# A gated recurrence beside weight products: contributions in 64x64 array tiles and a gather by ScalarE

## The reference

```
q, k, log_f, v -> chunks of C = 32 tokens
b       = cumsum(log_f) in the chunk;  b_mid, b_last
scores  = (q * exp(b - b_mid)) @ (k * exp(b_mid - b))^T, lower triangle
o_intra = scores @ v
contrib = (k * exp(b_last - b))^T @ v             # 64 x 64 per chunk
decay   = exp(b_last)
state_n+1 = decay_n * state_n + contrib_n;  o_inter = (q * exp(b)) @ state_n
o = rmsnorm(o_forward + o_backward, norm_g) * silu(g)
```

## Time and profile before

| what | us |
|---|---|
| median of three runs | 1155.03 |
| the profiled execution | 1154.56 |
| its span, first to last instruction | 1152.7 |
| TensorE busy with matmuls | 1142.7 (99%) |
| VectorE busy | 621.3 (54%) |
| ScalarE busy | 455.0 (39%) |
| GpSimd busy | 82.2 (7%) |

### The profile page before, as it was taken

How to read it: one execution, slowest core, us unless ns; L and a number is a source line. 1 busy time by engine, 2 the same in 40 slices (tenths; PEclk the granted TensorE clock), 3 DMA queues, 4 the chain that set the end, 5 groups by cost and what they waited for, 6 DMA issues and landing times.

```text
span 1152.7 us, 16038 instructions
## 1 busy us (share of the span) xinstructions
PE 1142.7 (99%) x6071; PEld 922.9 (80%) x6071; DVE 621.3 (54%) x776; ACT 455.0 (39%) x682; POOL 82.2 (7%) x74
## 2 busy tenths in 40 slices
PE   9999999999999999999999999999999999999997
PEld 7888888888888777666788788888888888888886
DVE  6755555553333685444588956655455555542223
ACT  6423223232222445555757655534423223232223
POOL 0000000000001120000044320020000000000000
PEclk9999999999999999999999999999999999999999
DMA  6332232233323341211131122423232232232221
GB/s 206 110 109 92 90 109 91 98 126 100 101 86 130 127 132 58 71 55 55 55 111 39 57 74 92 164 94 108 92 109 91 91 109 87 95 102 99 92 92 73
DMA packets 31679, 111.59 MB, mean 97 GB/s; under 512 B 3984, under 2 KB 5136, under 8 KB 31376
## 3 DMA queue, kind: packets, MB, share of 16 engines
q1 hardware_dynamic: 30192, 104.11, 27.2%
q10 hardware_dynamic: 1440, 6.82, 1.6%
HBM read 105.41 MB, written 4.19 MB: 95 GB/s over the span
## 4 chain that ended last, share of the span: by engine, by line
PE 95%; DVE 2%; issue 1%; ACT 1%; DMA 0%; POOL 0%; ACTq 0%; DVEq 0%; POOLq 0%
PE ps L1166 26%; PE ps L1168 26%; PE ps L1167 26%; PE ps L1202 3%; PE ps L1201 3%; PE ps L1200 3%; PE ps L1306 1%; PE ps L1317 1%; PE ps L1332 1%; DVE w_lo L766 0%; PE ps L1461 0%; DVE k_sc L766 0%; DMA raw<-up_dram 0%; PE ps L1437 0%; PE ps L1366 0%
## 5 line engine op out<-in xcount | busy, mean ns | idle before, releaser
L1166 PE MATMUL ps<-h_hi,w_hi 128*128 128x512 f32 x1024 | 407.1, 398 | 0.0
L1168 PE MATMUL ps<-h_hi,w_lo 128*128 128x512 f32 x1024 | 398.9, 390 | 0.0
L1167 PE MATMUL ps<-h_lo,w_hi 128*128 128x512 f32 x1024 | 398.8, 389 | 0.0
L766 DVE TENSOR_TENSOR w_lo<-raw,w_hi 128x1024 fp32r<-128x1024 f32 (+2 forms) x190 | 236.1, 1245 | 191.9 <-ACT w_hi L411 185.7
L411 ACT ACTIVATE w_hi<-raw 128x1024 fp32r<-128x1024 f32 (+1 forms) x182 | 196.2, 1080 | 173.0 <-PE ps L1168 96.0
L1166 PEld LDWEIGHTS ps<-h_hi,w_hi 128*128 128x128 f32 x1024 | 192.2, 188 | 55.0 <-issue 15.8
L1167 PEld LDWEIGHTS ps<-h_lo,w_hi 128*128 128x128 f32 x1024 | 192.3, 188 | 41.6 <-issue 2.9
L1168 PEld LDWEIGHTS ps<-h_hi,w_lo 128*128 128x128 f32 x1024 | 192.2, 188 | 40.4
L481 ACT ACTIVATE g_hi<-un 128x512 f32 (+1 forms) x44 | 27.8, 632 | 250.8 <-DVE un L766 250.8
L766 DVE TENSOR_TENSOR un<-ps,rs 128x512 f32<-128x512 f32 x44 | 30.4, 691 | 122.2 <-PE ps L1168 122.2
L1166 PE MATMUL ps<-g_hi,w_hi 128*128 128x512 f32 x176 | 68.5, 389 | 0.0
(11 more groups left out here) (241 smaller groups left out, 1188.0 us busy)
## 6 DMA issues: line engine op xcount, KB each, us to landing
raw<-up_dram SPq DMA_DIRECT2D x86, 512.0 KB, 3.2
raw<-proj_dram SPq DMA_DIRECT2D x26, 512.0 KB, 3.2
raw<-down_dram SPq DMA_DIRECT2D x16, 704.0 KB, 4.1
raw<-down_dram SPq DMA_DIRECT2D x22, 512.0 KB, 3.2
raw<-gates_dram SPq DMA_DIRECT2D x16, 512.0 KB, 3.2
raw<-branch_dram SPq DMA_DIRECT2D x8, 512.0 KB, 3.2
raw<-wout_dram SPq DMA_DIRECT2D x8, 512.0 KB, 3.2
x_spill_dram<-xT ACTq DMA_DIRECT2D x1, 2048.0 KB, 7.0
```

The costliest lines, as they stand in the source:

```text
L766: return V.tensor_tensor(out, a, b, op)
L1166: T.matmul(ps[:, bank, :], w_hi[:, slot, cols], moving_hi(j), start=start and j == 0, stop=False)
L1167: T.matmul(ps[:, bank, :], w_hi[:, slot, cols], moving_lo(j), start=False, stop=False)
L1168: ins = T.matmul(ps[:, bank, :], w_lo[:, slot, cols], moving_hi(j), start=False, stop=stop and j == tiles - 1)
```

## The change

The zeros in `k_nat` go: one buffer, filled by one copy of 128 partitions from bank 7. contributions takes 64 rows of tokens by 64 columns and writes banks 6 (even super-chunks) and 7 (odd), dense. A new ScalarE step, contributions_to_sbuf, copies both halves into `con_sb` in the interleaved order, and the scan reads that. The step is placed ahead of exponentials(u+2). On ScalarE keys_to_sbuf moves ahead of norm_exp; on VectorE query_key of the even tiles from 4 on moves between the first and second product of normalize; on GpSimd the far queries become a step of their own behind key_to_end, and gate_outputs waits until the queries for the edges are made. The output banks are 4 and 5.

```diff
-        k_nat = [at("k_nat0", 80, [P, ST, P]), at("k_nat1", 88, [P, ST, P])]
+        k_nat, con_sb = at("k_nat", 80, [P, ST, P]), at("con_sb", 88, [P, HD * NSUP])
-        OUT_BANKS = (5, 7)
+        OUT_BANKS = (4, 5)
 # GpSimd
             def query(u):
-                pool.wait_ge(qs_done, u + 1)
-                pool.wait_ge(fac_done, u + 1)
-                late = 1 - u % 2
-                nc.gpsimd.tensor_tensor(kq_far[:, :, late, :], ...).then_inc(qfar_done, 1)
+            def far_query(u):
+                late = 1 - u % 2
+                pool.wait_ge(qs_done, u + 1)
+                nc.gpsimd.tensor_tensor(kq_far[:, :, late, :], ...).then_inc(qfar_done, 1)
-            for masked in k_nat:
-                nc.gpsimd.memset(masked[:], 0.0).then_inc(zero_done, 1)
                 query(u + 1)
                 key_to_end(u + 1)
+                far_query(u + 1)
                 if u and u % 2 == 0:
+                    pool.wait_ge(qe_done, 2 * u + 4)
                     gate_outputs(u // 2 - 1)
 # ScalarE, keys_to_sbuf
-                for b, tokens in enumerate(head_rows):
-                    A(k_nat[b][tokens, :, :].rearrange("p j c -> p (j c)"), ps[tokens, 6, :], ACT.Copy).then_inc(kn_done, 1)
+                A(k_nat[:].rearrange("p j c -> p (j c)"), ps[:, 7, :], ACT.Copy).then_inc(kn_done, 1)
+
+            def contributions_to_sbuf(u):
+                act.wait_ge(con_done, u + 1)
+                if u:
+                    act.wait_ge(state_done, u)
+                A(con_sb[:].rearrange("p (e j b) -> p b j e", j=ST, b=2),
+                  ps[:, 6:8, 0:S // 2].rearrange("p b (j e) -> p b j e", e=HD), ACT.Copy).then_inc(ccp_done, 1)
...
             keys_to_sbuf(0)
             exponentials(1)
+            contributions_to_sbuf(0)
...
+                if u + 1 < TILES:
+                    keys_to_sbuf(u + 1)
                 if u and u % 2 == 0:
                     norm_exp(u // 2 - 1)
-                if u + 1 < TILES:
-                    keys_to_sbuf(u + 1)
...
                 if u % 2:
                     outputs_to_sbuf(u // 2)
+                if u + 1 < TILES:
+                    contributions_to_sbuf(u + 1)
                 if u + 2 < TILES:
                     exponentials(u + 2)
 # VectorE
                 link(stt(o_u[:], o_u[:], -0.5, o_ms[:], ALU.mult, ALU.mult))
+                if u is not None:
+                    query_key(u)
                 link(stt(o_rs[:], o_u[:], 1.5, o_rs[:], ALU.add, ALU.mult))
...
-                dve.wait_ge(con_done, u + 1)
+                dve.wait_ge(ccp_done, u + 1)
-                con, flat = ps[:, 4, :], ...
+                con, flat = con_sb[:], ...
...
-                if odd and u + 1 < TILES:
+                if u == 1:
                     query_key(u + 1)
...
-                    normalize(t - 1)
+                    normalize(t - 1, u + 2 if u + 2 < TILES else None)
 # TensorE
             def mean_square(t):
-                pe.wait_ge(kn_done, 2 * min(2 * t + 3, TILES))
+                pe.wait_ge(ccp_done, min(2 * t + 3, TILES))
             def key_transposes(u):
-                if u >= 3 and u % 2:
-                    pe.wait_ge(oeps_done, u // 2)
                 if u:
-                    pe.wait_ge(kn_done, 2 * u)
+                    pe.wait_ge(ccp_done, u)
-                    ins = T.transpose(ps[:, 6, ...
+                    ins = T.transpose(ps[:, 7, ...
             def contributions(u):
-                pe.wait_ge(kn_done, 2 * u + 2)
+                pe.wait_ge(kn_done, u + 1)
-                if u:
-                    pe.wait_ge(state_done, u)
+                if u >= 3:
+                    pe.wait_ge(oeps_done, (u - 1) // 2)
-                    j = n // 2
+                    j, tokens = n // 2, head_rows[n % 2]
-                        ins = T.matmul(ps[rows, 4, :].rearrange("p (e n) -> p e n", n=NSUP)[:, :, n],
-                                       k_nat[n % 2][:, j, HD * a:HD * (a + 1)], v_h[:, j, HD * h:HD * (h + 1)], start=True, stop=True)
+                        ins = T.matmul(ps[rows, 6 + n % 2, HD * j:HD * (j + 1)],
+                                       k_nat[tokens, j, HD * a:HD * (a + 1)], v_h[tokens, j, HD * h:HD * (h + 1)], start=True, stop=True)
```

More of the change, by code:

```diff
@@ L219, in build @@
         sc_done, scm_done, kt_done, kn_done = sem("sc_done"), sem("scm_done"), sem("kt_done"), sem("kn_done")
-        zero_done, con_done, state_done = sem("zero_done"), sem("con_done"), sem("state_done")
+        zero_done, con_done, ccp_done, state_done = sem("zero_done"), sem("con_done"), sem("ccp_done"), sem("state_done")
         o_done, osq_done, oms_done = sem("o_done"), sem("osq_done"), sem("oms_done")
@@ L338, in query @@
                 nc.gpsimd.tensor_tensor(q_sc[:], q_sc[:], hq[:, u // 2, :], ALU.mult).then_inc(qs_done, 1)
-                pool.wait_ge(qs_done, u + 1)
-                pool.wait_ge(fac_done, u + 1)
-                late = 1 - u % 2
-                nc.gpsimd.tensor_tensor(kq_far[:, :, late, :], supers(q_sc[:])[:, :, CHUNK * late:CHUNK * (late + 1)],
-                                        far_q[:, u % 2, :].unsqueeze(2).to_broadcast([P, NSUP, CHUNK]), ALU.mult).then_inc(qfar_done, 1)
             def key_to_end(u):
@@ L355, in key_to_end @@
                                         .to_broadcast([P, 2 * NSUP, CHUNK]), ALU.mult).then_inc(ke_done, 1)
+            def far_query(u):
+                late = 1 - u % 2
+                pool.wait_ge(qs_done, u + 1)
+                nc.gpsimd.tensor_tensor(kq_far[:, :, late, :], supers(q_sc[:])[:, :, CHUNK * late:CHUNK * (late + 1)],
+                                        far_q[:, u % 2, :].unsqueeze(2).to_broadcast([P, NSUP, CHUNK]), ALU.mult).then_inc(qfar_done, 1)
             def gate_outputs(t):
@@ L367, in _ @@
             key_to_end(0)
+            far_query(0)
             pool.wait_ge(sil_done, HH)
             pool.wait_ge(pv_done, PAIRS)
-            for masked in k_nat:
-                nc.gpsimd.memset(masked[:], 0.0).then_inc(zero_done, 1)
             pool.wait_ge(spilled, 16)
@@ L672, in keys_to_sbuf @@
                     act.wait_ge(con_done, u)
-                else:
-                    act.wait_ge(zero_done, 6)
-                for b, tokens in enumerate(head_rows):
-                    A(k_nat[b][tokens, :, :].rearrange("p j c -> p (j c)"), ps[tokens, 6, :], ACT.Copy).then_inc(kn_done, 1)
+                A(k_nat[:].rearrange("p j c -> p (j c)"), ps[:, 7, :], ACT.Copy).then_inc(kn_done, 1)
[5 more added lines that the diff above has]
+                  ps[:, 6:8, 0:S // 2].rearrange("p b (j e) -> p b j e", e=HD), ACT.Copy).then_inc(ccp_done, 1)
             def outputs_to_sbuf(t):
@@ L684, in outputs_to_sbuf @@
                     for j, from_rows in enumerate(head_rows):
-                        A(out[:, :, j, :, :], ps[from_rows, OUT_BANKS[0]:OUT_BANKS[1] + 1:2, P * a:P * (a + 1)]
+                        A(out[:, :, j, :, :], ps[from_rows, OUT_BANKS[0]:OUT_BANKS[1] + 1, P * a:P * (a + 1)]
                           .rearrange("p b (q c) -> p q b c", c=SUPER), ACT.Copy).then_inc(ocp_done, 1)
@@ L1023, in cumulate, with normalize @@
                 tt(chunks(k_sc[u % 2][:]), b3, mid.unsqueeze(2).to_broadcast([P, 2 * NSUP, CHUNK]), ALU.subtract).then_inc(d1_done, 1)
-            def normalize(t):
+            def normalize(t, u=None):
                 dve.wait_ge(oy_done, t + 1)
                 link(stt(o_u[:], o_u[:], -0.5, o_ms[:], ALU.mult, ALU.mult))
+                if u is not None:
+                    query_key(u)
                 link(stt(o_rs[:], o_u[:], 1.5, o_rs[:], ALU.add, ALU.mult))
@@ L1075, in scan_states @@
                 turn = slice(None, None, -1 if u % 2 else 1)
-                con, flat = ps[:, 4, :], state[u % 2][:].rearrange("p e n -> p (e n)")
+                con, flat = con_sb[:], state[u % 2][:].rearrange("p e n -> p (e n)")
                 V.tensor_tensor_scan(flat[:, turn], decay[u % 2][:, turn], con[:, turn], 0.0, ALU.mult, ALU.add).then_inc(state_done, 1)
@@ L1398, in key_transposes @@
                 pe.wait_ge(ke_done, u + 1)
-                if u >= 3 and u % 2:
-                    pe.wait_ge(oeps_done, u // 2)
                 if u:
-                    pe.wait_ge(kn_done, 2 * u)
+                    pe.wait_ge(ccp_done, u)
                 for j in range(ST):
-                    ins = T.transpose(ps[:, 6, P * j:P * (j + 1)], k_end[:, P * j:P * (j + 1)], ident)
+                    ins = T.transpose(ps[:, 7, P * j:P * (j + 1)], k_end[:, P * j:P * (j + 1)], ident)
                 ins.then_inc(kt_done, 1)
```

## The result

The changed kernel is slower, not faster: a median of 1160.2 us over 5 runs (1159.3 to 1160.67) against 1154.86 for the kernel before on the same chip. The ratio is 1.0045 with a 95% interval of [1.0034, 1.0055], so 5.3 us more where 4.8 less were forecast. Its profiled execution has a span of 1158.4 us against 1152.7: 5.7 more. The predicted time and its range were missed, on the other side of no change. Medians and ranges here are those of undisturbed executions; one of e4's ten took 2324.3 us and is left out.

The account below looks back on a forecast made before the run. TensorE, 99% busy, was taken as the bound. Gains of 2.70 + 0.29 + 0.49 + 1.63 = 5.11 us less 0.3 of new wait gave 4.8 net, from 1155.03 to a median of 1150.2 us; range 1148.8 to 1153.4.

Parts of the forecast that it names:

- Contributions on TensorE: The 64x64 contributions in the recurrence gain 0.46 us in tile 0 and 0.32 in each of seven others, 2.70 together.
- Rival B: Change of matmul form eats the contributions' gain in all tiles; 2.1 us gained, 1152.9 us; chance 0.14.
- The second copy of the keys: One 128-partition key copy ahead of norm_exp removes TensorE's waits for `k_nat` in tiles 0, 2 and 4: 0.78 us.
- The wait for `k_end`: query_key inside normalize makes `k_end` ready near 631.4, removing TensorE's waits in tiles 3 and 5: 1.63 us.
- The copy: ScalarE's new contributions_to_sbuf, 128x512 per tile, takes 0.60 us and stays hidden from TensorE.
- hidden, by 0.6: mean_square, wanted at 618.76, finds ScalarE's copy done by 618.2, so it does not wait.
- What is late next: VectorE: VectorE's run to the end of scan_states(3) ends at 633.77, a new wait of 0.3 us before outputs(3), bounds 0 to 1.5.
- the split: VectorE's split beside GpSimd's multiplication took 2.20 instead of 1.2; with gate_outputs held back, that 1.0 us goes.
- the last two products of normalize: VectorE's two products beside GpSimd's queries, 1.02 against 0.69 each, are spared some 0.7 us.
- Once only: The 0.3 us wait occurs only before outputs(3); outputs(5) has a whole gate unit before it, outputs(7) no cumulation.
- C: VectorE and ScalarE become the bound: slow forms stay, copy takes 1.0; 2.0 us lost, 1151.9 us; chance 0.16.
- D: ScalarE's strided copy is slow and delays exponentials and transposes; eats the 4.8 us gain at 1.9; chance 0.08.

Follow-up runs that it names:

- e4: Changed kernel with mask copy of odd tiles ahead of normalize, their scan inside it behind query_key, yb_hi and yb_lo moved: 1156.03 us, ratio 1.0013.
- e2: Kernel before with only the three moves (keys_to_sbuf, query_key, far queries with gate_outputs' wait); 128-row contributions and PSUM scan kept: 1155.6 us, ratio 1.0008.
- e5: Changed kernel with ScalarE's gather turned round, reading PSUM strided and writing con_sb densely, same result: 1158.5 us, ratio 1.0033.
- e3: Changed kernel with the gather dense on both sides in PSUM's order, leaving out the re-ordering, so states are mixed up: 1158.48 us, ratio 1.0037.
- e8: Changed kernel with scan_states reading one PSUM word repeatedly instead of con_sb, leaving contributions out of the states: 1157.62 us, ratio 1.0024.
- e1: Changed kernel with its three moves undone; 64x64 contributions, ScalarE's gather and scan from SBUF stay: 1159.73 us, ratio 1.0042.

## Why the prediction was wrong

**Contributions on TensorE, 2.70: right.** 1.15 to 0.69 from first start to last end in tile 0, 2.11 to 1.79 for the stretch behind. Rival B is out: the change of form in front cost no more than the missing overlap that the sum had counted.

**The second copy of the keys, 0.78: right.** No wait for `k_nat` is left in the kernel after.

**The wait for `k_end`, 1.63: right for the move alone** (e2 has none), wrong together with the rest. The key product of tile 4 was to stand near 629 and stood at 630.09, and took 1.30; `k_end` was there at 632.75, not 631.4.

**The copy, 0.60: mis-sized,** 1.2 measured. Its cost to the whole is the difference to e5, 1.5 us by the medians, and is not what turned the sign. With it fell the "hidden, by 0.6" of mean_square: the copy ended at 617.98 and mean_square began at 618.12, 0.23 late, and so in three tiles (0.7 in all); with a copy of 0.60 (e3, e5) it is on time.

**"What is late next: VectorE" is the step that failed,** twice over.

First, its size. "The scan reads SBUF instead of PSUM: I take its 1.21", I wrote, as if the place of the operand were nothing. A VectorE product of two SBUF operands and a product of GpSimd don't run side by side, and the rows of before had it: the split took 2.20 beside GpSimd's product, the scan out of PSUM 1.21 beside `k_end` (and better at 620.77, in the rows of before that stand above). I used that rule to remove 1.0 from the split, and did not apply it to the scan that the change had just made an instruction of two SBUF operands. The scan grew by 0.87, the subtraction beside the held gate_outputs by 0.92 (that product had not gone, it had moved), the key product by 0.6, and a new wait inside normalize added 0.4. Against that the split lost 0.6 and not 1.0, the far keys 0.3, and the last two products of normalize 0.1 and not 0.7: I had misread them, they took 1.67 and 0.99 us before and take 1.53 and 0.99 after. In sum the run to the masks grew by 1.7, where I had it shrink by 1.0. (The sum itself gives 633.77 - 633.53 = 0.24, which I had rounded up to 0.3.)

The same rule works the other way too, on a step that the prediction moved and put at nothing. The far queries now stand on GpSimd behind `k_end`, where they meet that scan: they took 1.53 us in most tiles of after and 0.61 in e2, where the scan reads PSUM, and TensorE lost 1.2 us before the far scores. A gather of 0.60 brings them early enough in that order (e3, e5).

The Trainium skill (SBUF — State Buffer, Who interferes with whom) states the rule: an instruction of VectorE with two SBUF inputs and one of GpSimd that reads SBUF contend, the first to issue has the shared port pair for the whole instruction, and the other blocks; with at most one SBUF input, outside VectorE's two-port modes, there is no contention. This case's traces agree: 2.07 against 1.21 for the same scan beside the same product (e8). It was the rule that spoke against this change, and I had weighed two others.

Second, the place of the wait. I asked which is late for outputs(3), the scan. Ahead of it stands chunk_scores(4), which waits for mask_scores(3), and query_key had been in front of that copy. Moving query_key ahead of two products of normalize gives the transposes early and leaves the masks where they are: a hole of 1.8 in tiles 3 and 5 both. That this place of the wait counts by itself is seen in e2 (2.2 us of mask waits, with no slow scan) and in e4, where the masks come early and 4 of the 5.3 us go. What the slow scan is worth is seen in e8, where 2.4 of the 5.3 go. "Once only" was wrong for the same reason, since the scores of tile 6 stand before the second gate unit of tile 5.

**What no step had** is the clock: 2.6 us of the profiled execution. A hole also costs what the matmuls behind it lose at the lower level, where it falls. In e1, e3 and e8 it fell behind both large holes, in the kernel after behind the second alone though the first was as long, in e5 behind the first alone, in e4 behind the second, and in e2 (0.91 and 1.26) behind none. What decides is not isolated here; that executions of one kernel differ in it, and that the spread of e5 (1156.28 to 1160.84) comes from it, is argued and not shown. Nor is it shown how much of e4's and e8's gain is clock and how much is wait.

**The rivals.** C (VectorE and ScalarE become the bound) had the right mechanism with 0.16, but 2.0 us of cost where 10.5 were paid. D had the side, by another cause: it needed a copy of 1.9, the copy took 1.2, where its formula gives 0.5, and with a copy of 0.60 (e5) 3.9 of the 5.3 were still lost. The rule of the Trainium skill that was weighed there (SBUF — State Buffer, Door 1), that each access that crosses to a new 16-byte line pays, agrees in direction: words written 32 bytes apart cost twice the time, 1.2 against 0.6.

## What to carry to other kernels

Before an operand moves from PSUM to SBUF, count the operands of every instruction that reads it and look what GpSimd does beside it: the second SBUF operand of a VectorE instruction can cost more than the copy (2.4 us in e8 against 1.5 in e5). When one of several steps on a full helper is moved forward, list every wait of the bound engine on that helper, in the engine's own order, since the hole moves to the next one. And compare forms in the order that suits each: with its helpers ordered well, the old form ran in 1152.5 us, 2.2 under the kernel before, and the form with the cheaper matmuls in 1153.6.

## What of the hardware was unexpected

- A VectorE instruction with two SBUF operands takes turns with GpSimd in whole instructions: 1.21 becomes 2.07 for the scan, 0.69 becomes 1.61 for a subtraction, and where VectorE was first GpSimd's product of 1.29 becomes 2.28 and its far queries of 0.61 become 1.53. With one operand in PSUM: 1.21 beside the same product.
- A ScalarE copy of 128x512 words that writes with a step of 32 bytes takes 1.2 us, one that reads PSUM with a stride and writes densely 0.60, as the dense one.
- Two holes of 2.7 us together, with the transposes between, in a stream of matmuls were followed by some 5.5 us of matmuls at a granted clock of 0.50, which cost 2.6 us: as much as the holes. The same two holes two tiles earlier, at 632.81 and 635.24 of the same execution, were followed by no fall of the clock.
- Not tried: 64x64 contributions with a scan out of PSUM. The two row groups write different banks, all eight are in use, and the scan as written goes over one row of 512 words.
